# Feed-forward loop: activations turned in 32 by 32 blocks on VectorE and moved by 16 transfers within SBUF, in place of TensorE transposes

## What is computed

```
h = rmsnorm(x, norm_ffn_g)                                    # 256 x 2048
x = x + (silu(h @ w_gate) * (h @ w_up)) @ w_down              # inner width 5632
return rmsnorm(x, norm_final_g)
```

## Time and profile before

| | |
|---|---|
| median of 3 runs | 1132.21 us (1132.09 to 1132.76) |
| the profiled execution | 1132.04 us, of which the span from first to last instruction is 1130.2 us |
| PE, DVE, ACT busy | 99%, 63%, 47% of the span |
| granted TensorE clock | 0.998 of full speed |
| the ten turns | about 457.7 us to 1101 us of the span |

### The profile page before, as it was taken

One profiled execution on the slowest core, in us unless ns is written; L12 is line 12 of the kernel. 1 busy time (PEld: TensorE's weight loads), 2 busy tenths in 40 slices (PEclk: granted clock), 3 DMA queues, 4 the chain that ended last, 5 costly groups with the idle time before them and its releaser, 6 DMA issues.

```text
span 1130.2 us, 15159 instructions
## 1 busy us (share of the span) xinstructions
PE 1116.9 (99%) x5618; PEld 925.8 (82%) x5618; DVE 714.2 (63%) x783; ACT 532.6 (47%) x640; POOL 88.3 (8%) x130
## 2 busy tenths in 40 slices
PE   9999999999999999999999999999999999999996
PEld 7878778888988888888888888888888888888885
DVE  7999998566765645464555546455554645556466
ACT  7569444345734553434343443444434343443443
POOL 7120234220000000000000000000000000000000
PEclk9999999999999999999999999999999999999999
DMA  9883688854665567566665656656566666656652
GB/s 362 285 237 115 203 247 261 229 170 149 237 210 197 171 204 215 188 192 186 191 198 186 188 188 195 188 188 196 187 192 186 191 190 193 188 186 201 186 187 93
DMA packets 115095, 224.81 MB, mean 199 GB/s; under 512 B 8432, under 2 KB 13936, under 8 KB 114416
## 3 DMA queue, kind: packets, MB, share of 16 engines
q1 hardware_dynamic: 110832, 214.05, 60.8%
q0 software_dynamic: 3808, 9.31, 3.2%
q10 hardware_dynamic: 416, 0.92, 0.2%
HBM read 218.09 MB, written 5.11 MB: 197 GB/s over the span
## 4 chain that ended last, share of the span: by engine, by line
PE 86%; DVE 8%; DMA 2%; issue 1%; ACT 1%; SPq 0%; POOL 0%; POOLq 0%; DVEq 0%; ACTq 0%
PE ps L1404 24%; PE ps L1406 24%; PE ps L1405 24%; PE ps L1442 3%; PE ps L1435 3%; PE ps L1439 3%; DVE w_lo L778 3%; DMA raw<-in_w_in 2%; PE ps L1651 1%; PE ps L1720 1%; PE ps L1722 1%; PE ps L1721 1%; PE ps L1550 0%; DVE cl_t L978 0%; DMA swapped<-state 0%
## 5 line engine op out<-in xcount | busy, mean ns | idle before, releaser
L778 DVE TENSOR_TENSOR w_lo<-raw,w_hi 128x1024 fp32r<-128x1024 f32 x384 | 467.8, 1224 | 383.0 <-ACT w_hi L442 382.0
L442 ACT ACTIVATE w_hi<-raw 128x1024 fp32r<-128x1024 f32 x383 | 406.0, 1061 | 563.8 <-PE ps L1406 456.2
L1404 PE MATMUL ps<-w_hi,actA_hi 128*128 128x512 f32 x416 | 162.9, 392 | 0.0
L1405 PE MATMUL ps<-w_lo,actA_hi 128*128 128x512 f32 x416 | 161.9, 389 | 0.0
L1406 PE MATMUL ps<-w_hi,actA_lo 128*128 128x512 f32 x416 | 161.9, 389 | 0.0
L1406 PE MATMUL ps<-w_hi,h2B_lo 128*128 128x512 f32 x352 | 137.0, 389 | 0.0
L1404 PE MATMUL ps<-w_hi,h2B_hi 128*128 128x512 f32 x352 | 136.9, 389 | 0.0
L1405 PE MATMUL ps<-w_lo,h2B_hi 128*128 128x512 f32 x352 | 136.9, 389 | 0.0
L1404 PE MATMUL ps<-w_hi,ffT_hi 128*128 128x512 f32 x320 | 124.6, 389 | 0.0
L1406 PE MATMUL ps<-w_hi,ffT_lo 128*128 128x512 f32 x320 | 124.5, 389 | 0.0
L1405 PE MATMUL ps<-w_lo,ffT_hi 128*128 128x512 f32 x320 | 124.5, 389 | 0.0
(11 more groups left out here) (265 smaller groups left out, 1294.1 us busy)
## 6 DMA issues: line engine op xcount, KB each, us to landing
raw<-in_w_gate SPq DMA_DIRECT2D x88, 512.0 KB, 3.7
raw<-in_w_up SPq DMA_DIRECT2D x88, 512.0 KB, 3.7
raw<-in_w_down SPq DMA_DIRECT2D x88, 512.0 KB, 3.6
raw<-in_w_in SPq DMA_DIRECT2D x79, 512.0 KB, 5.4
raw<-in_w_out SPq DMA_DIRECT2D x32, 512.0 KB, 4.3
k_tab<-k_scratch POOLq DMA_DIRECT2D x64, 64.0 KB, 3.7
raw<-in_ssm_w_glu SPq DMA_DIRECT2D x8, 512.0 KB, 3.4
x_tok<-in_x_tok SPq DMA_DIRECT2D x2, 1024.0 KB, 8.5
```

The lines of the kernel that those rows point to most:

```text
L442: nc.scalar.activation(w_hi[:, s % SPL], raw[:, s % RAW], ACT.Copy).then_inc(S["high_done"], 1)
L778: tt(w_lo[:, s % SPL], raw[:, s % RAW], w_hi[:, s % SPL].bitcast(F32), ALU.subtract).then_inc(S["low_done"], 1)
L1404: mm(o, x_hi, h, start=first, stop=False)
L1405: mm(o, x_hi, l, start=False, stop=False)
```

## The change

The 8 transposes of a turn go. In their place DVE turns `ff_act` in blocks of 32 by 32 within its partitions (`turn_blocks`, two instructions, into `ff_turned`); SP moves the 16 block rows and columns to their partitions by 16 transfers of 32 KB within SBUF (`ff_moved`, semaphore `d_moved`), one or two behind each weight load from c = 5 to c = 15; ACT and DVE then split `ff_moved` as before they split the PSUM result. The places move too: ACT's `ffT_high` from behind `high(11)` to behind `high(17)`, DVE's `ffT_low` from behind `low(11)` to behind `low(18)`. `turn_blocks` stands behind `low(20)`, right after `ff` of the group it turns. Before the loop one `turn_blocks` stands behind the `ff` of group 0. The last group keeps its TensorE transposes.

```diff
@@ SyncE, in the loop over turns
                     load(LOOP0 + c, src.rearrange("(b p) n -> p b n", p=P), turn=j)
+                    if 5 <= c < 16:
+                        if c == 5:
+                            sp.wait_ge(S["turned"], j + 1)
+                        for a, b in PAIRS[16 * (c - 5) // 11:16 * (c - 4) // 11]:
+                            sp.dma_start(ff_moved[32 * b:32 * b + 32, :, a].rearrange("p t k j -> p t (k j)"),
+                                         ff_turned[32 * a:32 * a + 32, b].rearrange("p t k j -> p t (k j)")
+                                         ).then_inc(d_moved, 16)
@@ ScalarE
             def ffT_high(count):
-                act.wait_ge(S["ffT_mm"], count)
-                nc.scalar.activation(ffT_hi[:].rearrange("p (a b) s -> p a (b s)", a=2), ps[:, 4:6], ACT.Copy
+                act.wait_ge(d_moved, count * MOVED)
+                nc.scalar.activation(turned_view(ffT_hi[:]), moved_view, ACT.Copy
                                      ).then_inc(S["ffT_hi_ready"], 1)
...
                     if c == GRP + SPL - 1:
+                        act.wait_ge(S["turned"], j + 1)
+                        silu(j * TURN + (LOOP0 + GRP))
+                    if c == GRP + SPL + 5:
                         ffT_high(j + 1)
-                        silu(j * TURN + (LOOP0 + GRP))
@@ VectorE
+            def turn_blocks(count, moved):
+                dve.wait_ge(S["ff_ready"], count)
+                if moved is not None:
+                    dve.wait_ge(d_moved, moved)
+                for t in range(TOK):
+                    last = nc.vector.transpose(ff_turned[:, :, t].rearrange("p b k j -> p k b j"),
+                                               ff_act[:, t].rearrange("p (k b j) -> p k b j", k=4, b=4))
+                last.then_inc(S["turned"], 1)
+
             def ffT_low(count):
                 dve.wait_ge(S["ffT_hi_ready"], count)
-                tt(ffT_lo[:].rearrange("p (a b) s -> p a (b s)", a=2), ps[:, 4:6],
-                   ffT_hi[:].rearrange("p (a b) s -> p a (b s)", a=2).bitcast(F32), ALU.subtract
-                   ).then_inc(S["ffT_lo_ready"], 1)
+                tt(turned_view(ffT_lo[:]), moved_view,
+                   turned_view(ffT_hi[:]).bitcast(F32), ALU.subtract).then_inc(S["ffT_lo_ready"], 1)
...
                     low(None, turn=j, at=LOOP0 + c)
-                    if c == GRP + 3:
+                    if c == GRP + SPL + 6:
                         ffT_low(j + 1)
                     if c == 2 * GRP + 3:
                         ff(j + 2, j * TURN + (LOOP0 + 2 * GRP))
+                    if not last and c == 2 * GRP + 4:
+                        turn_blocks(j + 2, (j + 1) * MOVED)
@@ TensorE
                     if c == GRP - 1:
                         pe.wait_ge(S["cols_added"], j * 4 + 8)
-                        ff_transposes(j + 1)
```

More of the change, by code:

```diff
@@ L127 @@
 SQUARES_AT = 8
+MOVED = 16 * 16
+PAIRS = [(a, b) for a in range(4) for b in range(4)]
 LAST_ORDER = tuple((t, slice(NCOL * c, NCOL * (c + 1))) for c, t in ((0, 0), (0, 1), (1, 0), (1, 1), (2, 0), (3, 0), (2, 1))
@@ L176, in build @@
         x2, state, swapped, kT, warm = (m[k] for k in ("x2", "state", "swapped", "kT", "warm"))
-        m = overlay([("qT", [P, HEADS, SEQ], F32)], [("u_tok", [P, TOK, 1024], F32)],
+        m = overlay([("qT", [P, HEADS, SEQ], F32)], [("ff_turned", [P, 4, TOK, 4, 32], F32), ("ff_moved", [P, TOK, 4, 4, 32], F32)], [("u_tok", [P, TOK, 1024], F32)],
                     [("cosA", [P, HALF, NCH], F32), ("sinA", [P, HALF, NCH], F32)])
@@ L181, in build @@
         ret = qT
+        ff_turned, ff_moved = m["ff_turned"], m["ff_moved"]
         m = overlay([("u_loc", [P, GROUPS, NCH], F32)],
@@ L276, in build @@
             "zT_ready sqT_ready ssm_hi ssm_lo sq_added ssq_mm ssq_ready cols_added last_added h2_mm h2_hi h2_lo x2_sq silu_ready ff_ready "
-            "ffT_mm ffT_hi_ready ffT_lo_ready fin_sq gain_done fin_ready fin1_ready last_mm"
+            "turned ffT_mm ffT_hi_ready ffT_lo_ready fin_sq gain_done fin_ready fin1_ready last_mm"
         ).split()
+        d_moved = sem("d_moved")
         S = {n: sem(n) for n in names}
@@ L339, in y_half, with turned_view @@
             return slice(2 * P * (b % 2), 2 * P * (b % 2 + 1))
+        moved_view = ff_moved[:].rearrange("p t a k j -> p (t a) k j")
+        def turned_view(x):
+            return x.rearrange("p k (c j) -> p c k j", j=32)
         def flat(x):
@@ L727, in turn @@
                     if c == GRP + SPL - 1:
+                        act.wait_ge(S["turned"], j + 1)
+                        silu(j * TURN + (LOOP0 + GRP))
+                    if c == GRP + SPL + 5:
                         ffT_high(j + 1)
-                        silu(j * TURN + (LOOP0 + GRP))
                     if last and c == 2 * GRP + 8:
-                        act.wait_ge(S["ffT_mm"], FG)
+                        act.wait_ge(S["ffT_mm"], 1)
                         nc.scalar.activation(ffE_hi[:].rearrange("p (a b) s -> p a (b s)", a=2), ps[:, 0:2], ACT.Copy
@@ L1178, in side @@
                     ff(1, LOOP0)
+                    turn_blocks(1, None)
             for n in range(LOOP0 + SPL):
```

## The result

The changed kernel takes 1135.28 us as a median of 8 runs (1134.56 to 1136.71), beside 1132.72 us for the kernel before, run with it (8 runs, 1132.01 to 1134.43). The ratio is 1.0026 with a 95% interval from 1.0018 to 1.0035: slower by 2.56 us, or 0.23%. The forecast was 1135.0 us and 0.25% slower.

A forecast was written before the change was run, and what follows sets the result against it. The prediction took PE's instruction stream as the bound: 1132.04 - 8.7 (transposes) + 11.5 (stall) = 1134.8 us for a profiled execution, with the median 0.17 above, so 1135.0 us, 0.25% slower; range 1132.5 to 1138.5.

The forecast's parts named there:

- What bounds the kernel: PE's own instruction stream, busy 99% of the span with no waits in the ten turns, sets the end.
- The transposes, 0.87 us a turn: Gain on PE from removing eighty of 88 transposes, priced by starts around them: 8.7 us for ten turns.
- rival 4: Removed transposes on PE save their listed time, 21.8 us, against 11.5 us of stall: 1121.9 us; chance 0.02.
- The stall, 1.15 us a turn: PE waits at chunk 16 because `ffT_low` behind `low(18)` ends 0.94 us late; 11.5 us for ten turns.
- The register term: Extra delay in nine of ten turns, where PE's wait at chunk 16 sits on a register instruction: 0.05 us assumed.
- The start 0.09 us ahead of the end of `low(18)`: On DVE, `ffT_low` starts before the `low` ahead of it ends; otherwise 0.9 us more over ten turns.
- Block turns, moves, `ffT_high` at no cost: Added work on DVE, SP and ACT was claimed to fit into existing slack, cost 0.
- The bound of 3.3 us behind `low(20)`: DVE's two block turns cost nothing up to 3.27 us together, before `down_col` is late for PE's chunk 20.
- Rival 2: `ffT_lo` is in time for PE's chunk 16, so 8.7 us are saved: 1123.5 us; chance 0.09.
- Rival 3: PE's stall at chunk 16 is only 0.65 to 0.87 us a turn: 1130 to 1132 us; chance 0.06.
- Rival 5: Slow block turns on DVE, from 1.6 us each, make `down_col` late for chunk 20: 1148 us at 2.3; chance 0.06.
- Rival 6: Moves delay weight loads by over 10 us, so PE waits for `low`; 1 us a turn gives 1145; chance 0.05.

## Why the prediction was right, step by step

**What bounds the kernel**: right. Every change to PE's stream, matmuls taken out or waits put in, came through in full.

**The transposes, 0.87 us a turn**: a turn of 66.18 us became 65.28 where nothing waits, so 0.90 us. With the wait gone, the median is 9.1 us under the kernel before, where 8.7 was forecast for ten turns. Their listed 272 ns each would have given 21.8 us (rival 4); the starts were the right thing to read.

**The stall, 1.15 us a turn**: the turns of the changed kernel and of the kernel with `ffT_low` one place earlier differ by 66.47 - 65.28 = 1.19 us, and the medians, each taken over its kernel before, by 11.7 for ten. Its parts, in the rows of the second turn: `ffT_low` ended 0.93 us late (forecast 0.94); the hand-over to PE took 546.88 - 546.75 = 0.13 us where 0.05 + 0.05 was put; the slow first matmul 0.10 (0.11). The register term, for which no row existed, can be told apart in the tenth turn, which has no such instruction. There `ffT_low` and PE stand so in the timeline:

```profile
1077.32 1.22 DVE L1129 TENSOR_TENSOR ffT_lo<-ff_moved,ffT_hi 128x1024 fp32r<-128x1024 f32 x1
```

```profile
1077.32 0.39 PE L1439 MATMUL ps<-w_hi,h2B_lo 128*128 128x512 f32 x1
1078.59 0.50 PE L1437 MATMUL ps<-w_hi,ffT_hi 128*128 128x512 f32 x1 [0.88 <-DVE ffT_lo L1129]
1078.93 0.40 PE L1438 MATMUL ps<-w_lo,ffT_hi 128*128 128x512 f32 x1
1079.17 0.40 PE L1439 MATMUL ps<-w_hi,ffT_lo 128*128 128x512 f32 x1
1079.41 0.40 PE L1437 MATMUL ps<-w_hi,ffT_hi 128*128 128x512 f32 x1
```

Released directly, PE starts 0.05 us after the end at 1078.54, as in the earlier trace rows. In the nine looped turns it is 0.12 or 0.13 us each time, and the kernel before with its `ffT_low` behind `low(18)` has the same split (nine of 0.12 or 0.13, and 0.06). So a release with the register instruction takes some 0.08 us longer, where 0.05 was put. The wait as a whole is only 0.02 us shorter in the tenth turn, since `ffT_low` ends 0.06 us later there against PE's last matmul; why, no run shows. One small part was missed: some of the matmuls behind the first one also start 0.24 us apart in place of 0.227, some 0.03 us together.

**The start 0.09 us ahead of the end of `low(18)`**: right (545.53 against 545.62). The prediction took from the Trainium skill (VectorE: DVE Perf Modes, The DRAIN you can't avoid) that the next instruction doesn't start until the pipe is empty; the same paragraph goes on to say that one which is not held starts earlier, and the trace agrees with that. Read whole, then, the page doesn't ask for the 0.9 us that the prediction worked out from it.

**Block turns, moves, `ffT_high` at no cost**: right, shown by the kernel without the first two, and for `ffT_high` (1.044 us in a slot of 1.66) by ACT's `high(18)` in the changed kernel, which still finds 0.71 us idle time before PE releases it:

```profile
541.54 1.04 ACT L735 ACTIVATE ffT_hi<-ff_moved 128x1024 fp32r<-128x1024 f32 x1
543.29 1.06 ACT L460 ACTIVATE w_hi<-raw 128x1024 fp32r<-128x1024 f32 x1 [0.71 <-PE ps L1439]
```

The bound of 3.3 us behind `low(20)` lies between the two tried: four block turns (2.4 us) fit under it, eight (4.8 us) do not. One size was wrong without consequence: a move holds SP for 0.60 us, not 0.37, so two cost 1.2 of its 4.8 us of slack. In the first turn SP is held for 7.6 us where 5.5 was foreseen, and ACT then waits for weights, 3.4 us at the longest; PE doesn't wait.

**Rivals.** Rival 2, the gain that stands, is what one place earlier gives. Rival 3, half a stall, is what the kernel with two halves shows. Rival 5's mechanism is real, but it takes more than four block turns of 0.6 us each, not two slow ones. Rival 6 is ruled out by the kernel without moves, which is no faster. None of the text's prices weighed the clock; at a wait of 1.2 us a turn that was right (granted clock 0.997), and one chunk later it would have been wrong by 18 us.

**Sum**: 10 x (1.19 - 0.90) = 2.9 us against 2.6 measured and 2.8 forecast. The mechanism is shown, but that the net comes out within 0.2 us is in part luck: it is the difference of two terms of some ten us, and their errors, 0.4 us in the stall and 0.3 us in the transposes, nearly cancel. That the time itself is met within 0.3 us is so too: the kernel before ran 0.5 us above the median that the forecast started from.

## What to carry to other kernels

Where one engine is busy throughout, price a removed instruction by the starts around it, and then look for the instruction that ends each wait of that engine and where it stands in its own queue. Work that runs ahead by chunks is released by chunks: each place later in the order moves its end by a whole chunk (2.72 us here), and what PE loses is the part that lies behind the due time (nothing behind `low(17)`, 1.19 us behind `low(18)`, over 3.8 us behind `low(19)`). So count its end against the due time before moving it "as late as possible". A change of place that looks free because 19 us of slack lay there before can use up all of it and 1 us more.

## What was not expected of the hardware

- The granted clock of TensorE stayed at full speed through gaps of 1.29 us between two starts in each turn (1.00 in the windows of the turn, 0.997 over the changed kernel), and of 1.66 us with eight block turns (0.998). With gaps of 4.0 us it fell to its lower level, 1.2 GHz, in every turn. With it the kernel took 18.5 us more than the waits alone would give, and its runs scatter by 16 us. The Trainium skill (TensorE: Matmul & The Clock Gate, section Why this matters for your kernels) warns that long idle gaps between bursts of matmuls bring the clock down; the trace agrees for those of 4.0 us.
- PE starts 0.12 or 0.13 us after the end of the DVE instruction where a register instruction carries the wait, and 0.05 or 0.06 us after it where none does. Behind such a wait the first two matmuls start 0.32 to 0.34 us apart, the next ones 0.23 to 0.24, before they are back at 0.227.
- A transfer of 32 KB within SBUF holds SP for 0.60 us, longer than a load of 512 KB (0.37 us), and lands after 3.5 us (medians of the changed kernel's trace).
- Block turns of 512 float32 elements on VectorE start 0.60 us apart (four in 2.40 us in the kernel with eight) and are listed with 0.69 us each.
